# Two transformer blocks on one Trainium2 core: the large SBUF tensors are placed at multiples of 2048 bytes

## The reference, cut to what matters

```python
def swiglu(h, w_gate, w_up, w_down):
    return (jax.nn.silu(h @ w_gate) * (h @ w_up)) @ w_down
# layer 0: proj = h @ w_in; MLA and stick-breaking attention; o @ w_o
# layer 1: proj = h @ w_in; 16 heads of attention with decay;  o @ w_o
# second block: xn @ w_in, (g_a*y_a + g_b*y_b) @ w_out, cross attention, then per expert
        xb = xt[tok]
        hb = jax.nn.silu(xb @ w1[e]) * (xb @ w3[e])
        return hb @ w2[e]
```

## Time and profile before

| | us |
|---|---|
| median of three runs | 2667.7 (2666.65 to 2680.87) |
| the profiled execution | 2678.92 |
| its span, first to last instruction | 2677.2 |
| TensorE matmuls busy (12026) | 2586.1 |
| VectorE busy | 1515.3 |
| ScalarE busy | 1241.2 |
| mean granted TensorE clock | 0.974 of full speed |

### The profile page before, as it was taken

How to read it: one execution, slowest core, us unless ns; L and a number is a source line. 1 busy time by engine, 2 the same in 40 slices (tenths; PEclk the granted TensorE clock), 3 DMA queues, 4 the chain that set the end, 5 groups by cost and what they waited for, 6 DMA issues and landing times.

```text
span 2677.2 us, 30191 instructions
## 1 busy us (share of the span) xinstructions
PE 2586.1 (97%) x12026; PEld 2098.2 (78%) x12026; DVE 1515.3 (57%) x2029; ACT 1241.2 (46%) x1598; POOL 112.5 (4%) x163
## 2 busy tenths in 40 slices
PE   8999999999999999999999999989998999999995
PEld 6767878888787787888887778878886888888884
DVE  5558544344434754434457454354356888888885
ACT  4468332123435742212323333333344777778773
POOL 0111000000140000000000000000001000000001
PEclk9959999999998999999999999999999999999997
DMA  4300332423331033252333022321306999999993
GB/s 147 121 1 1 110 111 95 157 95 126 135 118 40 1 101 98 97 170 91 114 109 112 32 103 94 110 95 63 128 1 249 426 425 408 409 406 404 408 404 134
DMA packets 158437, 431.72 MB, mean 161 GB/s; under 512 B 11067, under 2 KB 82902, under 8 KB 145878
## 3 DMA queue, kind: packets, MB, share of 16 engines
q1 hardware_dynamic: 150262, 400.35, 40.3%
q10 hardware_dynamic: 4736, 16.81, 1.5%
q0 software_dynamic: 3296, 12.58, 1.3%
HBM read 382.53 MB, written 47.19 MB: 161 GB/s over the span
## 4 chain that ended last, share of the span: by engine, by line
PE 89%; DVE 5%; ACT 2%; issue 2%; DMA 1%; POOL 0%; ACTq 0%; POOLq 0%; DVEq 0%
PE ps L314 19%; PE ps L315 19%; PE ps L316 19%; PE ps L2712 6%; PE ps L2710 6%; PE ps L2711 6%; PE ps L996 1%; PE ps L2692 1%; PE ps L1678 1%; PE ps L1971 1%; PE ps L1651 1%; PE ps L962 1%; PE ps L2120 1%; DVE area L339 1%; PE ps L2739 1%
## 5 line engine op out<-in xcount | busy, mean ns | idle before, releaser
L316 PE MATMUL ps<-area,area 128*128 128x512 f32 (+2 forms) x1712 | 663.4, 387 | 0.0
L339 DVE TENSOR_TENSOR area<-area,area 128x2048 fp32r<-128x2048 f32 (+4 forms) x161 | 340.9, 2118 | 560.0 <-ACT area L333 560.0
L333 ACT ACTIVATE area<-area 128x2048 fp32r<-128x2048 f32 (+4 forms) x161 | 284.3, 1767 | 564.2 <-PE ps L316 559.1
L315 PE MATMUL ps<-area,area 128*128 128x512 f32 (+3 forms) x1368 | 529.2, 387 | 0.0
L2680 DVE TENSOR_TENSOR area<-area,area 128x2048 fp32r<-128x2048 f32 x192 | 433.3, 2284 | 62.9 <-ACT area L2675 62.0
L314 PE MATMUL ps<-actT_parts,area 128*128 128x512 f32 (+1 forms) x984 | 389.9, 396 | 6.8 <-DVE area L339 2.8
L315 PE MATMUL ps<-actT_parts,area 128*128 128x512 f32 (+1 forms) x984 | 388.5, 395 | 0.0
L316 PEld LDWEIGHTS ps<-area,area 128*128 128x128 f32 (+1 forms) x1712 | 320.7, 187 | 70.7
L2675 ACT ACTIVATE area<-area 128x2048 fp32r<-128x2048 f32 x192 | 360.7, 1913 | 20.3 <-PE ps L2712 16.4
L315 PEld LDWEIGHTS ps<-area,area 128*128 128x128 f32 x1368 | 258.3, 189 | 52.3
L314 PE MATMUL ps<-area,area 128*128 128x512 f32 (+2 forms) x728 | 277.0, 381 | 3.5 <-DVE area L737 3.5
(11 more groups left out here) (347 smaller groups left out, 3228.7 us busy)
## 6 DMA issues: line engine op xcount, KB each, us to landing
area<-in_w SPq DMA_DIRECT2D x96, 2048.0 KB, 10.1
area<-in_w_in SPq DMA_DIRECT2D x16, 2048.0 KB, 7.8
area<-in_l_w_gate SPq DMA_DIRECT2D x22, 1024.0 KB, 5.4
area<-in_l_w_up SPq DMA_DIRECT2D x22, 1024.0 KB, 7.9
expert_inputs<-maskz SPq DMA_DIRECT2D x39, 512.0 KB, 8.6
area<-in_l_w_in SPq DMA_DIRECT2D x9, 2048.0 KB, 8.3
expert_rows<-area ACTq DMA_DIRECT2D x32, 512.0 KB, 9.2
area<-expert_inputs SPq DMA_DIRECT2D x31, 512.0 KB, 9.9
```

Source lines behind the costliest of these rows:

```text
L315: pe.matmul(dst(r), a.l, b.h, start=False, stop=False)
L316: m = pe.matmul(dst(r), a.h, b.l, start=False, stop=end)
L333: eng.activation(w.h, raw, ACT.Copy).then_inc(w_hi, 1)
L339: dve.tensor_tensor(w.l, raw, w.high_f, ALU.subtract).then_inc(w_lo, 1)
```

## The change

The small tables now come first, then a pad up to the next multiple of 2048 bytes, then `xT`, `actT` and the arena, whose lengths before it are multiples of 2048. The two head norm weights of layer 0 (`qg`, 768 bytes) no longer have a tensor of their own; they lie in the arena, where the setup stage reads them. The arena grows from 171520 to 171776 bytes. No instruction is added or removed, and the order on every engine stays as it is; two small loads (48 KB each) and the eight products of 64 columns that build the rotary tables name another place for `qg`.

```diff
-        xT = sb("xT", [P, KD, S])
         def sb_twice(name, shape):
 
             plain = sb(name, shape)
             at = nc.sbuf_base - 4 * int(np.prod(shape[1:]))
             return plain, nc.alloc_sbuf_tensor_at(name + "_parts", shape, F32R, offset=at)
 
-        actT, actR = sb_twice("actT", [P, KD, S])
-        orow = actT[:, :, :].rearrange("p (t a) s -> p t (a s)", t=NT)
         ident = sb("ident", [P, P])
...
-        qg = sb("qg", [P, 2, QK])
...
-        free = (nc.sbuf_bytes_remaining // 4 - 64) // 64 * 64
+        def align(to):
+            words = -nc.sbuf_base % to // 4
+            if words:
+                sb(f"pad{nc.sbuf_base}", [P, words])
+        align(2048)
+        xT = sb("xT", [P, KD, S])
+        actT, actR = sb_twice("actT", [P, KD, S])
+        orow = actT[:, :, :].rearrange("p (t a) s -> p t (a s)", t=NT)
+        free = (nc.sbuf_bytes_remaining // 4 - 16) // 64 * 64
         sb("arena", [P, free])
...
+        qg = work(A0 + 11392, 2, QK)
```

## The result

| | before | changed |
|---|---|---|
| median | 2674.28 us (4 runs) | 2639.78 us (4 runs) |
| spread | 2666.65 to 2688.07 | 2636.87 to 2642.65 |
| the profiled execution | 2678.92 | 2636.87 |
| its span | 2677.2 | 2635.2 |

The ratio is 0.9865, with a 95% interval of 0.9817 to 0.9914: 34.5 us faster at the medians, where 35 were forecast. (A fourth run of before, 2688.07 us, moved its median from 2667.7; the forecast time of 2633 us stood on the older one, and 2639.8 us is 7 above it.)

The account below looks back on a forecast made before the run. TensorE's pace was taken as the bound, slowed by operands at different positions; the trio terms summed to 36.2 us, 35 after hand-overs, so 2667.7 − 35 = 2633 us. Own range 2618 to 2643; 8 in 10, 2618 to 2654.

Parts of the forecast that it names:

- What bounds it: Whole kernel: TensorE, busy 2586 of 2677 us, is the bound; only its pace can move the time, and only addresses change.
- Two classes of trios by relative position: TensorE's trios of matmuls: 226.7 ns a matmul with operands at equal positions, 4 to 7 ns more at different ones.
- Different positions modulo 128 bytes (64 counts, 512 does not): Moving and stationary operands of the trios: the slow pace comes when their addresses differ modulo 128 bytes.
- The terms of the sum: TensorE time given back, by kind of trio: 15.7, 9.5, 9.7 and 1.3 us, 36.2 us in all.
- moving activations: 968 trios with activations as moving operand: 2904 matmuls, 5.4 ns saved on each, 15.7 us (12.5 to 19.2).
- Stationary: 608 trios with activations as stationary operand: 1824 matmuls, 5.2 ns saved on each, 9.5 us.
- What lies on the path: The trios' time is practically all on the chain; 1 us off for hand-overs leaves a gain of 35 us.
- The short matmuls: Some 3000 shorter matmuls and transposes on TensorE: taken as 0 gain, with up to 15 us kept for the range.
- DMA: Experts' weight loads: costed at nothing, 414 GB/s needed; rival that DMA holds the experts, gain 24 us, 2644, chance 0.11.
- Addresses are free: Rival on TensorE's trios: pace does not depend on operand positions; gain 0, 2668 us; chance 0.12.
- Equal positions collide: Rival on TensorE's trios: reads at equal positions meet in the same memory part; 23 us slower, 2691; chance 0.04.
- Alignment gives more: Rival: a quarter of the 32 cycles beyond 512 columns goes too, 30 us more, 2603; chance 0.04.

Follow-up runs that it names:

- arena_96: The changed kernel with 96 bytes of padding between `actT` and the arena; 2666.12 us, ratio 0.9999 to the kernel before.
- min_pad: The kernel before, its order of tensors untouched, with 32 bytes of padding ahead of the arena; 2637.50 us, ratio 0.9877.
- arena_128: The changed kernel with 128 bytes of padding between `actT` and the arena; 2657.54 us in one run.
- act_back_256: The changed kernel with `xT` and `actT` 256 bytes further forward, the arena where it was; 2636.34 us in one run.
- all_96: The changed kernel with 96 bytes of padding ahead of `xT`, so `actT` and the arena move alike; 2640.42 us, ratio 0.9896 to the kernel before.
- row_1088: The changed kernel with layer 1's attention output chunks at a stride of 4352 bytes instead of 4160; 2640.91 us, ratio 0.9894 to the kernel before.
- arena_32: The changed kernel with 32 bytes of padding between `actT` and the arena; 2666.78 us in one run.

## Why the prediction was right

*What bounds it*, right. Only addresses changed, and only TensorE's pace moved: VectorE busy 1515.1 us against 1515.3, the same counts on all engines.

*Two classes of trios by relative position*, right in kind. `arena_96` takes the whole gain back with 96 bytes and no other difference; `min_pad` gets it with 32 bytes that move the arena alone.

*"Different positions modulo 128 bytes (64 counts, 512 does not)"*: this step failed in its number. Rows 3 and rows 7 only said that the unit lies above 64 bytes and divides 512, so 128, 256 and 512 were all open; I took the first. `arena_128` is slow, `act_back_256` is fast: the unit is 256. It cost nothing in the forecast, since the change makes `actT` and the arena agree modulo 2048, which holds under each of the three.

*The terms of the sum*: 33.3 us given back of 36.2. The largest miss is the moving activations, 13.8 against 15.7: the middle of the two stretches of rows 4 (232.1 ns) was taken where the mean over all such matmuls was 231.7, and 0.8 us stay as transitions behind waits. Stationary (9.2 for 9.5), gate and up (9.0 for 9.7) and down (1.1 for 1.3) miss by little. Layer 1's output projection kept its 231.7 ns.

*What lies on the path*: 35 forecast, 34.5 measured at the medians. The interval of the ratio, 23 to 49 us, does not prove it so exactly; `min_pad`, with more runs and the same excess, gave 32.0 us (24 to 41). `all_96` gave 29.1 and `row_1088` 25.0 us at the medians, with nearly the same excess, so that the close meeting of 34.5 and 35 is in part luck: the median of before was the highest in that comparison (2674.28; 2667.02, 2669.47 and 2665.89 in the later ones). Over all the runs on record, the mean is 2668.7 us for 31 later ones of before and 2639.1 for 20 of the kernels with equal positions (the changed one, `min_pad`, `all_96`, `row_1088` and the two with `actT` further forward): 29.6 us. Their mean granted clocks are 0.9789 and 0.9771, and among the runs of before 0.01 of clock goes with 23 us. By an estimate from these numbers some 4 us of the 33 are lost in time at the lower clock; why the clock is granted less often, no run shows.

*The short matmuls*, taken at 0: eight transposes still take 0.89 us against 0.88. But with the unit of 256 the changed kernel does not test this, since `ident` lies 128 bytes past a multiple of 256 and the arena on one. In `min_pad` both lie at 128, and the eight take as long as before:

```profile
2120.59 0.88 PE ps L2693 x8
```

From start to start these transposes take 109.4 ns there, 111.2 in the changed kernel and 109.8 in the one before, so equal positions are worth 2 ns at most, under 2 us over all 860 full transposes with `ident`. The 15 us kept for the range were not there.

*DMA*: the rival did not come. The experts' period fell to 17.76 us, forecast 17.73, and the queues delivered 415 GB/s. On the packets the Trainium skill (DMA: Bandwidth & Descriptors, "How a descriptor splits into AXI transactions") gives the ones off a 256-byte boundary one transaction more; it says nothing of their time. The experts' weights come in 12288 packets of 16384 bytes. Their median is 611 ns in the changed kernel (at the boundary), in `all_96` and in the kernel before (both 96 bytes past it) alike. Their means, 629.6, 629.7 and 638.2, go with the experts' pace and not with the boundary. No run here shows the extra transaction.

*Addresses are free*: refuted by `arena_96`. The Trainium skill (SBUF — State Buffer, "Who interferes with whom") states that PE never waits on anyone. If that is read as covering TensorE's own two reads, these traces do not agree: the same matmuls take 226.7 ns or 233.3, by the operands' relative position. *Equal positions collide*: refuted, they are the fast ones. *Alignment gives more*: `all_96` and `min_pad`, off every boundary, have the same 226.7 ns as the changed kernel, so the 32 cycles beyond the 512 columns do not hang on where a pair that agrees lies (tried at 0, 96 and 128 bytes past a multiple of 2048).

## What to carry to other kernels

Where TensorE is the bound, read the distances between starts of equal matmuls in the timeline, not their durations: 4 to 7 ns in 227 do not show in a busy share and were 33 us here. If they fall into classes by tensor, compare the byte addresses of the moving and the stationary operand modulo 256, the row strides inside a tensor included; a pad of 32 bytes can be the whole cure. All this was seen for fp32r matmuls of 512 columns, each with new weights; for other types and for reused weights nothing was run. Two profiled executions of kernels can differ by more than the change does: compare the granted clock stage by stage before giving their difference a cause.

## What the runs showed that I had not expected

- The unit of 256 bytes, and that the cost is no steady function of the offset: 64 bytes cost most with moving activations (234.2 ns) and little in the gate and up products (228.7), 128 bytes the reverse (229.2 and 232.7).
- The fast pace is the same 226.7 ns wherever the operands lie, as long as they agree: 544 cycles for 512 columns.
- A matmul can be slowed by the one behind it: with `low_x` 128 bytes off and stationary, the distance before the unequal matmul grew from 226.7 to 232.5 ns. And the slow pace can outlast its cause, by six matmuls in the kernel before and by none in `arena_32`.
- The granted clock in one stage of the same work: 0.80 in one execution and 0.93 in another, 15 us.
